# A transformer-like network on one core: two RMS-norm chains, the last squared tile summed by TensorE in halves and the first scaled tile handed on in halves

## The reference, cut to what matters

```python
def rms_norm(x, g):
    y = x * lax.rsqrt(jnp.mean(x * x, axis=-1, keepdims=True) + EPS)
    return y * g

# first block, layer 0 (attention, Fourier mixing) ends, layer 1 (short convolution) begins
x = x + gate * even_output(...)
h = rms_norm(x, norm_g[1]) * (1.0 + scale) + shift
x = x + gate * short_conv_mixer(h @ odd_w_in, ...)
...
# second block: pooling mixer, then the convolutional feed-forward
x = x + pool_mixer(rms_norm(x, norm_mix_g), ...)
f = conv_ffn(rms_norm(x, norm_ffn_g), ...)      # h @ w_in, conv over rows, silu gate, @ w_out
x = x + f
```

## Time and profile before

| | |
|---|---|
| median of 3 runs | 1875.22 us (1873.84 to 1877.40) |
| the profiled execution, its own time | 1876.28 us |
| its span in the profile | 1874.5 us |
| PE busy | 1773.6 us, 95% of the span |
| DVE, ACT, POOL busy | 62%, 43%, 40% |
| mean granted TensorE clock | 0.982 of full speed |

### The profile page before, as it was taken

The page is one execution under the profiler, slowest core; times in us unless marked ns, Lnnn a source line. Parts: engine busy times, 40 slices in busy tenths (PEclk is TensorE's granted clock), DMA queues, the critical chain, the costliest instruction groups (busy, mean ns, idle before and its releaser), DMA issues.

```text
span 1874.5 us, 22911 instructions
## 1 busy us (share of the span) xinstructions
PE 1773.6 (95%) x8733; PEld 1475.4 (79%) x8733; DVE 1162.8 (62%) x1312; ACT 811.0 (43%) x1244; POOL 750.6 (40%) x458
## 2 busy tenths in 40 slices
PE   5899999889999599889999999998999999999999
PEld 3688888658888588778888888977888888878887
DVE  3703975348888633875454563488566666679876
ACT  5324221446766521633333342645444444444443
POOL 0325322000000033476666531257999999920000
PEclk9999999999999899899999999989999999999999
DMA  8414122540000280212222341312222322187433
GB/s 321 147 51 117 42 68 79 227 169 1 0 0 1 68 270 23 68 57 78 69 70 65 109 161 45 93 43 68 79 90 79 90 80 90 57 296 265 141 118 123
DMA packets 162088, 188.31 MB, mean 100 GB/s; under 512 B 9230, under 2 KB 117319, under 8 KB 160839
## 3 DMA queue, kind: packets, MB, share of 16 engines
q1 hardware_dynamic: 161991, 187.00, 30.2%
HBM read 152.37 MB, written 34.60 MB: 100 GB/s over the span
## 4 chain that ended last, share of the span: by engine, by line
PE 52%; DVE 3%; ACT 2%; DMA 1%; issue 1%; SPq 0%; POOL 0%; ACTq 0%; DVEq 0%; POOLq 0%
PE ps L2874 19%; PE ps L1923 13%; PE ps L2924 10%; PE ps L1979 5%; PE ps L3216 1%; PE ps L1935 1%; PE ps L2887 1%; DVE up_lo_p L130 0%; PE ps L1942 0%; PE ps L2891 0%; DMA res_scratch<-x_nat 0%; ACT residual L3059 0%; DMA w_raw<-in_ffn_w_out 0%; DMA y_a<-y_scratch 0%; DVE cv_lo_p L130 0%
## 5 line engine op out<-in xcount | busy, mean ns | idle before, releaser
L2874 PE MATMUL ps<-up_hi_p,st_hi_p 128*128 128x512 f32 x560 | 218.8, 391 | 5.8 <-ACT residual L2614 5.2
L2874 PE MATMUL ps<-up_lo_p,st_hi_p 128*128 128x512 f32 x560 | 218.4, 390 | 0.0
L2874 PE MATMUL ps<-up_hi_p,st_lo_p 128*128 128x512 f32 x560 | 218.3, 390 | 0.0
L2924 PE MATMUL ps<-down_ring 128*128 128x512 f32 x924 | 210.9, 390 | 0.9 <-DVE down_ring L130 0.8
L2924 PEld LDWEIGHTS ps<-down_ring 128*128 128x128 f32 x924 | 173.0, 188 | 38.6 <-issue 1.6
L130 POOL TENSOR_TENSOR in_lo<-in_raw,in_hi 128x512 fp32r<-128x512 f32 (+1 forms) x56 | 93.4, 1678 | 230.3 <-ACT in_hi L127 180.3
L130 POOL TENSOR_TENSOR st_lo_p<-up_raw,st_hi_p 128x512 fp32r<-128x512 f32 x68 | 142.7, 2102 | 97.9 <-ACT st_hi_p L127 97.9
L1923 PE MATMUL ps<-cv_hi_p,cv_st_hi_p 128*128 128x512 f32 x420 | 163.7, 390 | 5.1 <-issue 2.6
L1923 PE MATMUL ps<-cv_hi_p,cv_st_lo_p 128*128 128x512 f32 x420 | 163.4, 389 | 0.0
L1923 PE MATMUL ps<-cv_lo_p,cv_st_hi_p 128*128 128x512 f32 x420 | 163.4, 389 | 0.0
L2738 DVE TENSOR_TENSOR residual<-ps,residual 128x512 f32<-128x512 f32 x100 | 68.9, 689 | 105.2 <-PE ps L2874 105.2
(11 more groups left out here) (363 smaller groups left out, 4117.3 us busy)
## 6 DMA issues: line engine op xcount, KB each, us to landing
up_raw<-in_ffn_w_in SPq DMA_DIRECT2D x44, 512.0 KB, 5.1
w_raw<-in_ffn_w_out SPq DMA_DIRECT2D x66, 256.0 KB, 2.9
ada_raw_rest<-in_ada_w SPq DMA_DIRECT2D x32, 512.0 KB, 5.4
cv_raw<-in_odd_w_in SPq DMA_DIRECT2D x32, 512.0 KB, 5.5
in_raw<-in_even_w_in SPq DMA_DIRECT2D x48, 256.0 KB, 2.8
y_scratch<-residual SPq DMA_DIRECT2D x22, 512.0 KB, 2.6
ada_raw<-in_ada_w SPq DMA_DIRECT2D x8, 1024.0 KB, 16.8
residual<-in_x SPq DMA_DIRECT2D x2, 2048.0 KB, 10.4
```

The costliest lines, as they stand in the source:

```text
L2874: last = pe.matmul(ps[:, bank(j, p), :], w[p][:, kk * P:(kk + 1) * P], x[p][:, kk, :], start=(first and w is st_hi and x is up_hi), stop=( ...
L2924: last = pe.matmul(ps[:, 4 * (i % 2) + m, :], slot[:, s, m * P:(m + 1) * P], slot[:, x, :], start=(k == 0 and s == 0 and x == 2 and DOWN[i ...
```

## The change

Four things are done, at both chains where not said otherwise.

1. Tile 7's square is not added to total 1 by VectorE. TensorE multiplies it with the ones itself, 8 more products (24 in place of 16), in two halves of 4, each of which waits for the square of its half. Total 1 is complete with tile 6.
2. The last residual tile is made final in halves: in even_out the last output tile is computed LEFT first, then RIGHT (24 products each, as many as before); in the pooling the LEFT half is reported after banded(7)'s fourth block. VectorE adds, and ScalarE squares, two halves of 128x512 in place of one 128x1024. In VectorE's list the add of square 6 now stands ahead of the last residual tile.
3. The spread reports after 4 and after 8 transposes; tile 0 is scaled (in the convolution shifted, too) as two halves, and quarter p1 is split as soon as the left half is there. `scaled(4)` moves behind the low part of p1.
4. In the feed-forward only: turn(7) moves from ahead of TensorE's sum of squares to behind it (and so ahead of the spread). GpSimd's `ffn_pool_third` waits for tile 6's add in place of tile 7's.

```diff
@@ Norm.tensor_spread (the FFN's own ffn_spread likewise) @@
                     last = pe.transpose(self.rstd[:, r * P:(r + 1) * P], self.compact[:, r:r + 1].broadcast_to([P, P]),
                                         ident[:, :])
-                last.then_inc(self.s("spread"), 1)
+                    if (r + 1) % (self.n // P // parts) == 0:
+                        last.then_inc(self.s("spread"), 1)
@@ SquareSum @@
-            ON_POOL, ON_VECTOR = (2, 4), (3, 5, 6, 7)
+            ON_POOL, ON_VECTOR = (2, 4), (3, 5, 6)
+            DIRECT = KT - 1
...
+            def scalar_direct(self, act, side, half):
+
+                if side == 0:
+                    act.wait_ge(*self.summed(self.DIRECT - 2))
+                act.activation(self.buffers[self.DIRECT % 2][:, half], res[:, self.DIRECT, half], ACT.Square)\
+                   .then_inc(self.s("squared"), 1)
...
                     for r in range(RT):
-                        last = pe.matmul(self.mean[:, r:r + 1], square_totals[p][:, r * P:(r + 1) * P], ones[:, 0:1],
-                                         start=(p == 0 and r == 0), stop=(p == 1 and r == RT - 1))
+                        pe.matmul(self.mean[:, r:r + 1], square_totals[p][:, r * P:(r + 1) * P], ones[:, 0:1],
+                                  start=(p == 0 and r == 0), stop=False)
+                square = self.buffers[self.DIRECT % 2]
+                for r in range(RT):
+                    if r % (RT // 2) == 0:
+                        pe.wait_ge(self.s("squared"), KT + r // (RT // 2))
+                    last = pe.matmul(self.mean[:, r:r + 1], square[:, r * P:(r + 1) * P], ones[:, 0:1],
+                                     start=False, stop=(r == RT - 1))
@@ conv_scalar @@
                 for kk in range(HALF):
-                    shifted(kk, 2 * kk + 1)
-                    quarter_high("p1", kk)
+                    if kk == 0:
+                        shifted(0, 1, LEFT)
+                        quarter_high("p1", 0)
+                        shifted(0, 2, RIGHT)
+                    else:
+                        shifted(kk, 2 * kk + 2)
+                        quarter_high("p1", kk)
                     quarter_high("p5", kk)
@@ conv_vector (ffn_vector likewise) @@
-                dve.wait_ge(norm.s("spread"), 1)
                 dve.wait_ge(x1_spilled, 16 * (KT - len(SPILLED_LATE)))
+                for side, half in enumerate((LEFT, RIGHT)):
+                    dve.wait_ge(norm.s("spread"), side + 1)
+                    scaled(0, half)
                 for kk in range(HALF):
-                    scaled(kk)
-                    scaled(kk + HALF)
-                    quarter_low("p1", kk)
+                    if kk:
+                        scaled(kk)
+                        scaled(kk + HALF)
+                        quarter_low("p1", kk)
+                    else:
+                        quarter_low("p1", 0)
+                        scaled(HALF)
                     quarter_low("p5", kk)
@@ even_output: vector, tensor @@
-                        for m in range(KT):
+                        for m in range(KT - 1):
                             dve.wait_ge(sem("ow_done"), m + 1)
...
-                        squares.add(dve, KT - 1)
+                        squares.add(dve, KT - 2)
+                        for side, half in enumerate((LEFT, RIGHT)):
+                            dve.wait_ge(sem("ow_done"), KT + side)
+                            residual_added(KT - 1, half)
...
+                            for half in (LEFT, RIGHT) if m == KT - 1 else (slice(0, SEQ),):
+                                matmul3(pe, pair[m % 2][:, half], lambda k: w_hi[:, m % SLOTS, k, :], lambda k: w_lo[:, m % SLOTS, k, :],
+                                        lambda k, c, e: y_hi[:, k, half][:, c:e], lambda k, c, e: y_lo[:, k, half][:, c:e],
+                                        KT, half.stop - half.start).then_inc(sem("ow_done"), 1)
@@ ffn quarter_high @@
-                    act.wait_ge(sem("h_ready"), 2 * kk + (1 if p in ("p1", "p5") else 2))
+                    act.wait_ge(sem("h_ready"), 2 * kk + 2 - (p == "p1" and kk == 0) + (p in ("p2", "p3")))
@@ pooling: gpsimd, vector, tensor @@
-                        pool.wait_ge(*squares.summed(KT - 1))
+                        pool.wait_ge(*squares.summed(KT - 2))
                         ffn_pool_third(pool)
...
                         for m in range(KT):
-                            pool_add(m)
+                            if m < KT - 1:
+                                pool_add(m)
                             if m - 1 in squares.ON_VECTOR:
                                 squares.add(dve, m - 1)
-                        squares.add(dve, KT - 1)
+                        pool_add(KT - 1)
                         ffn_vector(dve)
...
+                                if m == KT - 1 and b == 3:
+                                    last.then_inc(sem("pool_done"), 1)
...
-                        turn(KT - 1)
                         pe.wait_ge(sem("res_copied"), 5)
                         squares.tensor(pe).then_inc(sem("res_meaned"), 1)
+                        turn(KT - 1)
                         pe.wait_ge(sem("res_copied"), 6)
                         ffn_spread(pe)
```

More of the change, by code:

```diff
@@ L212, in tensor_mean, with tensor_spread @@
                 last.then_inc(self.s("meaned"), 1)
-            def tensor_spread(self, pe):
+            def tensor_spread(self, pe, parts=1):
                 pe.wait_ge(self.s("inverse"), 1)
@@ L1949, in passes @@
                                  (up_hi[p][:, kk, :], up_lo[p][:, kk, :]), kk, first, stop)
-                norm.tensor_spread(pe)
+                norm.tensor_spread(pe, 2)
                 for kk in range(HALF):
@@ L2098, in _ @@
                                 early_scalar(act)
+                        for side, half in enumerate((LEFT, RIGHT)):
+                            act.wait_ge(sem("ow_added"), KT + side)
+                            squares.scalar_direct(act, side, half)
                     @block.gpsimd
@@ L2772, in product, with scaled @@
                     dve.tensor_tensor(vy[j % 2], vy[j % 2], gy, ALU.mult).then_inc(sem("fy_done"), 1)
-                def scaled(k):
-                    dve.scalar_tensor_tensor(out=res[:, k, :], in0=res[:, k, :], scalar=col(FFN_G, k), in1=pair[0],
+                def scaled(k, half=slice(0, SEQ)):
+                    dve.scalar_tensor_tensor(out=res[:, k, half], in0=res[:, k, half], scalar=col(FFN_G, k), in1=pair[0][:, half],
                                              op0=ALU.mult, op1=ALU.mult).then_inc(sem("h_ready"), 1)
@@ L2803, in ffn_vector @@
                 dve.reciprocal(ffn_compact[:, :], ffn_compact[:, :]).then_inc(sem("res_inverse"), 1)
-                dve.wait_ge(sem("res_spread"), 1)
+                for side, half in enumerate((LEFT, RIGHT)):
+                    dve.wait_ge(sem("res_spread"), side + 1)
+                    scaled(0, half)
                 for kk in range(HALF):
-                    scaled(kk)
-                    scaled(kk + HALF)
-                    quarter_low("p1", kk)
+                    if kk:
+                        scaled(kk)
+                        scaled(kk + HALF)
+                        quarter_low("p1", kk)
+                    else:
+                        quarter_low("p1", 0)
+                        scaled(HALF)
                     quarter_low("p5", kk)
@@ L3099, in _ @@
                         for m in range(KT):
-                            act.wait_ge(sem("pool_added"), m + 1)
-                            squares.scalar(act, m)
+                            if m < KT - 1:
+                                act.wait_ge(sem("pool_added"), m + 1)
+                                squares.scalar(act, m)
+                            else:
+                                for side, half in enumerate((LEFT, RIGHT)):
+                                    act.wait_ge(sem("pool_added"), m + side + 1)
+                                    squares.scalar_direct(act, side, half)
                             if m:
@@ L3182, in pool_add @@
                             dve.wait_ge(sem("bias_added"), m + 1)
-                            dve.wait_ge(sem("pool_done"), m + 1)
-                            dve.scalar_tensor_tensor(out=res[:, m, :], in0=pair[Z_PAIR[m % 4]], scalar=col(POOL_SCALE, m),
-                                                     in1=res[:, m, :], op0=ALU.mult, op1=ALU.add).then_inc(sem("pool_added"), 1)
+                            for side, half in enumerate((LEFT, RIGHT) if m == KT - 1 else (slice(0, SEQ),)):
+                                dve.wait_ge(sem("pool_done"), m + side + 1)
+                                dve.scalar_tensor_tensor(out=res[:, m, half], in0=pair[Z_PAIR[m % 4]][:, half], scalar=col(POOL_SCALE, m),
+                                                         in1=res[:, m, half], op0=ALU.mult, op1=ALU.add).then_inc(sem("pool_added"), 1)
                         conv_vector(dve)
```

35 lines of the change are left out of this document (18 added, 17 removed).

## The result

| | before | after |
|---|---|---|
| median, 20 runs each, taken together | 1876.81 us (1872.64 to 1882.32) | 1879.90 us (1876.51 to 1884.81) |
| ratio of the times | | 1.0019, 95% interval 1.0011 to 1.0027 |
| profiled execution, its own time | 1876.28 us | 1876.51 us |
| its span | 1874.5 us | 1874.7 us |

The change makes the kernel slower by 0.19%, some 3.6 us by the ratio: real, and just inside what the prediction called the same. The predicted 1876.2 was too low and the range, to 1879.4, ends half a microsecond under the measured median. A part of that lies in the foot of the sum: the kernel before took 1876.81 here, where three runs had given 1875.22.

A forecast was written before the change was run, and what follows sets the result against it. The prediction took the chain of waits through both norm chains into TensorE as the bound, with the clock's fall. Convolution -2.0 and feed-forward +2.9 gave about 1.0 us longer on 1875.22: 1876.2 us, range 1872.6 to 1879.4.

The forecast's parts named there:

- the foot of the sum: Whole kernel: the median before, 1875.22 us, to which the forecast added its 1.0 us.
- the halves were to win 2.0: Convolution: spread to first product in 3.1 us instead of 5.2, a gain of 2.0 us, bounds 1.7 and 2.2.
- the feed-forward had been +3.3: Feed-forward total against the profiled execution: 3.3 us late, taken as 2.9 against a usual run.
- a microsecond won ... before the first product should arrive at the end in full: Both chains: time won or lost before the first product reaches the end undiminished, one us for one.
- the prediction's own sign of being wrong: Convolution: large parts of the 2.0 us gain missing at the start of the long TensorE stretch (822.59 before).
- Convolution, the mean: Convolution sum of squares: the removed 2.16 us wait is eaten by 16 more instructions, 0.0 won; 0.9 won to 0.7 lost.
- the formula: Both chains: 48 one-column products take 10.7 - 0.97 G us, G being the time from their first to the clock's fall.
- Feed-forward, mean, turn and halves: Feed-forward before the first product: mean 2.3 us late, moved turn(7) 1.3 late, spread in halves 1.6 won.
- Feed-forward, GpSimd: Feed-forward, p2's low part: GpSimd 2.1 us later against TensorE with 0.9 to spare, so 1.2 to 1.3 late.
- a wait that would take both gains: Both chains: a wait binding both halves would cost the 2.0 and 1.6 us won; none seen, placed inside the slower case.
- The slower rival: Feed-forward's 48 products: an early clock fall before a late GpSimd, 5 us longer, 1880 us; chance 0.15.
- the rival drawn from it: Feed-forward: turns hold nothing, fall stays at 1220.1, mean 0.1 late, total -0.9 us; chance 0.20 shared with a late fall.

The follow-up runs named there:

- halves_only: Kernel before with only the spread and first tile in halves (part 3), in both chains; ratio 0.9997 to the kernel before.
- Experiments 2 and 4: Experiment 2 is the pair halves_only (0.9997) and sums_only (1.0005); experiment 4 is third_before_root_scaled4_first (1.0001).
- sums_only: Changed kernel with the halves of spread and first tile (part 3) undone in both chains; ratio 1.0005 to the kernel before.
- experiment 7: The run listed as best_of_both; ratio 0.9974 to the kernel before, median 1873.34 us.
- conv_only: The change at the convolution chain alone, feed-forward as before; ratio 0.9991 to the kernel before, median 1876.70 us.
- turn_moved_only: Kernel before with one edit, turn(7) moved behind the 32 one-column instructions; ratio 1.0007 to the kernel before.
- ffn_only: The change at the feed-forward chain alone, convolution as before; ratio 1.0025 to the kernel before, median 1881.70 us.
- third_after_root: Changed kernel, but ScalarE makes slot p3's high part right behind the root, ahead of the copy of turned tile 7; ratio 0.9998 to the kernel before.
- third_before_root_scaled4_first: Changed kernel with slot p3's high part ahead of the root and `scaled(4)` back ahead of p1's low part; ratio 1.0001 to the kernel before.
- totals_within_halves_third: Changed kernel: convolution totals' products between the last tile's large ones; feed-forward with original sums, halves, p3's high part ahead of the root; 0.9990 to before.
- best_of_both: Changed kernel with `scaled(4)` first in the convolution; feed-forward with original sums and turn, halves, p3's high part ahead of the root; 0.9974 to before.
- the change once more: The changed kernel run again unaltered, for its time and another draw of the clock; ratio 1.0022 to the kernel before.
- turn_back_third_before_root: third_before_root_scaled4_first with turn(7) back ahead of the sum of squares, and the convolution totals' products within the last tile; ratio 1.0021 to the kernel before.
- experiment 4: The run listed as third_before_root_scaled4_first; ratio 1.0001 to the kernel before.
- experiment 3: The run listed as third_after_root; ratio 0.9998 to the kernel before, median 1877.73 us.

## Why the prediction was wrong

**The shape held, in part by luck.** The two chains pull in opposite directions, the convolution wins and the feed-forward loses more, as the sum said (-2.0 and +2.9; measured -1.2 and +4.4). But the convolution's -1.2 is the result of two errors that nearly cancel: the halves were to win 2.0 and won 0.3, the mean was to win nothing and won 1.0. Against the profiled execution the feed-forward had been +3.3, so the errors are 0.8 and 1.1, both towards slower, and with the foot's 1.6 they carried the median out of the range.

**Convolution, "a microsecond won ... before the first product should arrive at the end in full".** This step failed. halves_only shows 1.78 us won at the first product (2.0 predicted) and 0.27 at the end. It is the prediction's own sign of being wrong, large parts of the 2.0 us missing where the long TensorE stretch begins. I had read the chain of waits as passing through TensorE from that product on. In the trace of before ScalarE, too, has no idle time between its first shift at 754.82 and the last of the plain quarters at 773.7, a shift and two splits in turn; when TensorE's first product came sooner this row came last, and its second shift had moved by a quarter of a microsecond. The prediction looked at quarter p2 and found it hidden by TensorE's half clock; it priced the moved `scaled(4)` against TensorE, not against ScalarE, which idled 0.67 us for it. Experiments 2 and 4 show both.

**Convolution, the mean.** Predicted 0.0 with G, the time from the first one-column product to the fall of the clock, at 3.2; the formula gives 6.9 us for the measured G of 3.9, and 6.66 were measured. sums_only won 1.02. The formula held; the G was wrong for this code. It was inside the bounds that were given, but the six further profiles with these 48 instructions behind the convolution's last tile all have 3.9 to 4.4, so the better term was about 0.9 won.

**Feed-forward, mean, turn and halves.** Counted from banded(7): the end of the one-column products 8.42 before and 10.97 after, 2.55 late (2.3 predicted, 2.9 by the measured G of 2.6); the spread's start another 0.9 late (1.3 predicted for the turn), since 12.58 against 9.10 makes 3.48; from spread to first product 2.65 in place of 4.07, 1.4 won (1.6). First product 15.23 against 13.17: 2.06 late, predicted 2.0. All of this was right to within half a microsecond.

**Feed-forward, GpSimd.** This is the term that was mis-sized: 1.2 to 1.3 late, bounds 0 to 1.8, and 2.2 were measured (p2's low part at 23.98 in place of 19.71, +4.27, of which the first product is 2.06). Its parts: the high part of slot p3 ended at 14.36 in place of 10.15, that is 2.15 later against the first product (2.1 predicted), and 1.05 was to spare, not 0.9: the prediction took half of a row of two, and the first of them ended at 1229.82. From that high part to p2's low part GpSimd then needed 9.6 us in place of 8.5: its low part and four sums 7.85 (1221.49 to 1229.34) in place of 7.2, the rest in p2's low part (1.71 in place of 1.29). The prediction's bound for this was that the sums might run *faster*, with VectorE idle beside them. They came to lie beside more of VectorE's work instead, and two of them ran at 1.75 and 1.84 us where experiment 7's early ones took 1.26. Which work slows them can be read off all 13 traces. VectorE's scaling does not: sums that had it beside them nearly throughout took 1.27 to 1.30. Its instructions with two operands in SBUF (TENSOR_TENSOR in the timeline, the splits above all) do. Of the 152 sums and low parts of 128x512 that GpSimd made between 1205 and 1245 us, the 85 in which such an instruction of VectorE ended, 0.46 us or more after their start, took 1.60 to 1.86 us, and the other 67 took 1.26 to 1.31, without an exception. That is a pattern over all the runs; no run changed it alone.

**What the halves then win is lost in a wait.** They were booked at 1.6. The prediction named a wait that would take both gains, saw none, and gave it no price of its own; there was one in each chain. Behind a late GpSimd they bring the first product forward and nothing else: F is 74.08 with and without them (sums_only). What F follows is the end of slot p3's high part, both counted from banded(7):

| run | wait for GpSimd | p3 high ends | F | difference |
|---|---|---|---|---|
| before | 0 | 10.15 | 69.72 | 59.6 |
| conv_only | 0.30 | 10.15 | 69.18 | 59.0 |
| halves_only | 2.23 | 10.21 | 69.90 | 59.7 |
| turn_moved_only | 1.28 | 11.67 | 71.26 | 59.6 |
| after | 2.91 | 14.36 | 74.08 | 59.7 |
| sums_only | 0.23 | 14.44 | 74.08 | 59.6 |
| ffn_only | 3.10 | 14.55 | 74.26 | 59.7 |
| third_after_root | 0.74 | 9.35 | 68.47 | 59.1 |
| third_before_root_scaled4_first | 0 | 7.42 | 67.81 | 60.4 |
| totals_within_halves_third | 0 | 6.32 | 67.42 | 61.1 |
| best_of_both | 0 | 6.32 | 67.12 | 60.8 |

With GpSimd in front the difference is 59.0 to 59.7, whatever the clock and the first product did; without a wait for it, F is longer than that row alone would make it. The kernel before belongs to the second kind though it shows 59.6, because its GpSimd was quick: counted from the end of p2's first low part, the seven runs with a wait have 50.2 to 50.5 left, before 51.1. The exceptions are the change once more (14.12 and 76.7, with the second fall) and turn_back_third_before_root (7.42 and 76.88), where half clock outlasted GpSimd.

**The profile and the runs.** C and F of the first profile give +3.2, the runs +3.6 and, a second time, +4.1 by the ratio. The second fall of the clock, behind a wait that the change introduced, was in no step of the prediction. It appeared in one of two profiles of the changed kernel. Falls behind such waits are common in these traces, though: 52 to 58 us behind layer 0's last product TensorE idles 2.6 us at full clock in each of the 13 profiles, and in eight the clock fell in this wait or within 1.5 us behind it; in four of the other five it fell within 1.1 us behind a wait of 2.3 us 22 us later. The kernel before is the one with neither, and C hardly sees these falls, since what comes behind them waits for VectorE in any case: it is 79.94 in turn_moved_only, with such a fall, against 79.96.

**The slower rival** gave the clock as its mechanism: G below 2 in front of a late GpSimd. The measured G was 2.6, 2.9 and 2.4 with the change's order, never under 2. The outcome came near that rival's 1880 by its second half alone.

**The rule on transposes.** The Trainium skill ("TensorE: Matmul & The Clock Gate", "Part 4: PE-mode transpose") counts transposes as not busy; the rival drawn from it had the fall at its old place 5.8 us behind the earlier start. The changed kernel's profiles show 2.6 and 2.9, sums_only and ffn_only 2.5 and 2.4; turn_moved_only, where turn(7) has moved as well, 5.0; third_after_root and the kernel of experiment 4 5.3. Counted from banded(7), the fall came after 8.2 to 9.5 us in the five profiles with turn(7) and the sums in their old places. In the seven with the turn behind the products it came after 8.1 to 8.4 us in three, near the old place, as that rule has it, and after 5.5 to 6.0 in four, which it does not give. So an early fall is seen only where the turn had moved, but twelve draws do not decide it.

**What stays open.** How often the second fall comes at this place: four profiles with the change's order show it once, and its wait was 2.67 us, and two others with 2.9 and 3.1 had none. That the halves, by lengthening the wait from 0.23 us to 2.9, invite it would explain why sums_only is quicker in time (1.0005) than the whole change (1.0019 and 1.0022) at the same F; but their intervals overlap (up to 1.0019, from 1.0011 and 1.0014), so that there may be nothing to explain, and no run tried it. And experiment 3's F was drawn with a late fall; only its time says that the order mended the loss, and a profile of it with an early fall is missing. Nor is it shown how often the late fall (5.3 us) comes.

## What to carry to other kernels

When a chain is cut shorter, follow each engine that feeds the operands after the first one, and ask which row comes next: here ScalarE's shifts were 0.3 us behind and GpSimd's sums one microsecond. Work that an engine owes to somebody else (slot p3's high part, with 9 us of GpSimd's behind it) belongs ahead of the chain, not inside; that reordering alone turned a loss of 0.2% into none; with the feed-forward's original sums and `scaled(4)` first in the convolution it became a gain of 0.26%. Count what more narrow products cost before using them to remove a wait. Sixteen more instructions took the place of a wait of 2.16 us in the convolution and won 1.0 there; in the feed-forward, where there was no wait, they made the mean 2.5 us late, since half of the 48 ran at half clock, at 0.223 us in place of 0.113.

## What the runs showed of the hardware

- From the first one-column product to the fall of the clock it was 2.4, 2.5, 2.6, 2.9, 5.0, 5.3 and 5.3 us in the feed-forward with turn(7) behind the products, 3.4 to 4.7 with it in front, and 3.2 to 4.4 in the convolution (without the two runs that have the totals inside the last tile). Where TensorE had idled 2.11 us ahead of the turn, it fell before the first of them. The prediction had 2.5 to 4.15.
- In one execution a wait of 2.67 us that began at full clock brought another fall and 6.8 us at half clock (1233.08 to 1239.91); in ffn_only 3.10 us of wait did not. Elsewhere waits of 2.3 to 2.6 us at full clock brought a fall in 12 of 18 cases.
- A 128x512 sum of two fp32 tiles on GpSimd took 1.26 us early in experiment 7 and up to 1.84 us in the changed kernel. It was slow where an instruction of VectorE with two operands in SBUF ended within it; one that scales out of PSUM beside it cost nothing.
- An fp32 product of one column costs two instructions of 0.12 us each even between large products: 3.8 us for 16 of them.
